# Gated-linear heads: the state update directly behind the scores, two stretches of projections per pair in place of three

## What is computed

```python
def gla_chunk(q, k, v, logf, s0):       # one chunk of L = 64 tokens
    b = jnp.cumsum(logf, axis=1)
    inter = jnp.einsum('blhk,bhkv->blhv', qf * jnp.exp(b), s0)
    decay = jnp.exp(jnp.where(causal, b[:, :, None] - b[:, None, :], -jnp.inf))
    attn = jnp.einsum('blhk,bmhk,blmhk->bhlm', qf, kf, decay)
    intra = jnp.einsum('bhlm,bmhv->blhv', attn, vf)
    k_dec = kf * jnp.exp(b_last[:, None] - b)
    s_new = jnp.exp(b_last)[..., None] * s0 + jnp.einsum('blhk,blhv->bhkv', k_dec, vf)
    return inter + intra, s_new
```

## Time and profile before

| | |
|---|---|
| median of three runs | 2609.63 us (2609.17 to 2614.47) |
| the profiled execution | 2610.18 us, of which its span is 2608.4 us |
| PE busy | 2502.8 us, 96% of the span |
| VectorE, ScalarE busy | 916.2 us (35%), 837.4 us (32%) |
| POOL busy | 552.7 us (21%) |
| granted TensorE clock | 0.986 of full speed on average |
| DMA | 53 GB/s over the span |

### The profile page before, as it was taken

How to read it: one execution, slowest core, us unless ns; L and a number is a source line. 1 busy time by engine, 2 the same in 40 slices (tenths; PEclk the granted TensorE clock), 3 DMA queues, 4 the chain that set the end, 5 groups by cost and what they waited for, 6 DMA issues and landing times.

```text
span 2608.4 us, 41617 instructions
## 1 busy us (share of the span) xinstructions
PE 2502.8 (96%) x17454; PEld 2363.0 (91%) x17454; DVE 916.2 (35%) x1793; ACT 837.4 (32%) x1658; POOL 552.7 (21%) x306
## 2 busy tenths in 40 slices
PE   6999999999999999999998999889999999999998
PEld 5888878798999999999997877688999999999997
DVE  6454454517322222222227344425422222222216
ACT  4445444536220221121125455536411211211212
POOL 1101110115221221211215210104312212211213
PEclk9999999999999999999999999899999999999999
DMA  3101010114111111111114100003211111111114
GB/s 108 41 10 48 22 44 17 44 45 150 61 45 41 48 40 48 40 48 40 53 40 141 62 26 26 30 27 121 84 41 49 40 48 40 48 40 41 47 53 134
DMA packets 63088, 139.05 MB, mean 53 GB/s; under 512 B 8688, under 2 KB 39920, under 8 KB 62960
## 3 DMA queue, kind: packets, MB, share of 16 engines
q1 hardware_dynamic: 33984, 103.60, 11.9%
q10 hardware_dynamic: 28976, 33.64, 4.2%
HBM read 117.81 MB, written 19.40 MB: 53 GB/s over the span
## 4 chain that ended last, share of the span: by engine, by line
PE 80%; DVE 3%; ACT 2%; issue 1%; ACTq 0%; DVEq 0%
PE banks L217 52%; PE banks L197 20%; PE banks L1903 1%; PE banks L1423 1%; PE banks L1404 1%; PE banks L1391 1%; PE banks L1431 1%; PE banks L2054 0%; PE banks L383 0%; PE banks L2057 0%; PE banks L2038 0%; ACT y L1557 0%; DVE y L614 0%; PE banks L1427 0%; PE banks L1385 0%
## 5 line engine op out<-in xcount | busy, mean ns | idle before, releaser
L160 POOL TENSOR_TENSOR w_lo<-w_raw,w_hi 128x1024 fp32r<-128x1024 f32 x168 | 414.9, 2473 | 1880.4 <-ACT w_hi L153 1880.4
L197 PE MATMUL banks<-h_hi,w_hi 128*128 128x384 f32 (+1 forms) x1224 | 430.0, 351 | 6.4 <-ACT gla_v_tok L2153 3.1
L197 PE MATMUL banks<-h_lo,w_hi 128*128 128x384 f32 (+1 forms) x1224 | 408.6, 334 | 0.0
L197 PE MATMUL banks<-h_hi,w_lo 128*128 128x384 f32 (+1 forms) x1224 | 408.2, 334 | 0.0
L153 ACT CAST w_hi<-w_raw 128x1024 fp32r<-128x1024 f32 x180 | 187.3, 1048 | 464.3 <-DMA w_raw<-in_units 464.0
L217 PE MATMUL banks<-h_hi,w_hi 128*128 128x384 f32 (+1 forms) x1368 | 301.7, 329 | 0.0
L217 PE MATMUL banks<-h_lo,w_hi 128*128 128x384 f32 (+1 forms) x1368 | 301.3, 328 | 0.0
L217 PE MATMUL banks<-h_hi,w_lo 128*128 128x384 f32 (+1 forms) x1368 | 301.3, 328 | 0.0
L217 PE MATMUL banks<-mlp_a_hi,w_hi 128*128 128x384 f32 (+1 forms) x1344 | 296.6, 329 | 1.5 <-issue 1.3
L217 PE MATMUL banks<-mlp_a_lo,w_hi 128*128 128x384 f32 (+1 forms) x1344 | 295.1, 327 | 0.0
L217 PE MATMUL banks<-mlp_a_hi,w_lo 128*128 128x384 f32 (+1 forms) x1344 | 295.0, 327 | 0.0
(11 more groups left out here) (201 smaller groups left out, 3175.9 us busy)
## 6 DMA issues: line engine op xcount, KB each, us to landing
w_raw<-in_units SPq DMA_DIRECT2D x180, 512.0 KB, 3.5
x_scratch<-y ACTq DMA_DIRECT2D x48, 192.0 KB, 2.0
norm_x<-x_scratch ACTq DMA_DIRECT2D x40, 192.0 KB, 2.6
x_scratch<-y ACTq DMA_DIRECT2D x24, 160.0 KB, 1.8
norm_x<-x_scratch ACTq DMA_DIRECT2D x20, 160.0 KB, 2.5
y<-in_x SPq DMA_DIRECT2D x16, 192.0 KB, 5.3
norm_x<-in_x ACTq DMA_DIRECT2D x16, 192.0 KB, 3.0
out_y<-y SPq DMA_DIRECT2D x16, 192.0 KB, 2.3
```

The source lines that it names most:

```text
L160: c.nc.gpsimd.tensor_tensor(c.w_lo[:, s], c.w_raw[:, s], c.w_hi[:, s].bitcast(F32), ALU.subtract).then_inc(self.ready, 1)
L197: mm = chip.nc.tensor.matmul(out, w, x, start=(first and n == 0), stop=(last and n == 2))
```

## The change

`update` moves directly behind `scores`; a pair has two stretches of projections, one between update and output and one behind the output. `STEPS`, `HIGHS` and ScalarE's places for `take_jobs` follow from that. On VectorE `states` moves from behind `differences(g + 2)` to directly behind `attention(g)`, and `output_variance` behind it.

```diff
-    PARTS = 3
+    PARTS = 2
-    STEPS = (PARTS * NPAIR, PARTS * NPAIR, PARTS * NPAIR, 21)
+    STEPS = (PARTS * NPAIR, PARTS * NPAIR, PARTS * NPAIR, 14)
-    HIGHS = ({2: 6, 4: 7, 10: 8, 15: 9}, {4: 4, 6: 5, 10: 6, 13: 7, 16: 8, 19: 9}, {4: 4, 6: 5, 10: 6, 13: 7, 16: 8, 19: 9},
-             {4: 4, 8: 5, 13: 6, 15: 7, 18: 8, 24: 9})
+    HIGHS = ({1: 6, 2: 7, 6: 8, 10: 9}, {2: 4, 4: 5, 6: 6, 8: 7, 10: 8, 12: 9}, {2: 4, 4: 5, 6: 6, 8: 7, 10: 8, 12: 9},
+             {2: 4, 5: 5, 8: 6, 10: 7, 12: 8, 16: 9})
...
                 scores(h, p)
+                update(h, p)
                 fill(h, self.PARTS * p)
-                update(h, p)
+                output(h, p)
                 fill(h, self.PARTS * p + 1)
-                output(h, p)
-                fill(h, self.PARTS * p + 2)
...
+                take_output(h, p)
+                if h and p == 0:
+                    scale_outputs(h, 2)
                 take_jobs(h, slot + 1)
                 if slot + 1 in self.HIGHS[h]:
                     ws.high(act, self.unit(h, self.HIGHS[h][slot + 1]))
-                take_output(h, p)
-                if h and p == 0:
-                    scale_outputs(h, 2)
-                take_jobs(h, slot + 2)
-                if slot + 2 in self.HIGHS[h]:
-                    ws.high(act, self.unit(h, self.HIGHS[h][slot + 2]))
...
                     nc.vector.memset(self.state[:, 0, 0], 0.0).then_inc(self.state_zero, 1)
-                    if h:
-                        output_variance(h)
+                states(h, p)
+                if h and p == 0:
+                    output_variance(h)
                 decayed(g + 1)
...
                 differences(g + 2)
-                states(h, p)
```

## The result

The changed kernel takes 2629.64 us (median of five runs, 2625.67 to 2634.69) against 2610.86 in the same comparison: 1.0071 times the kernel before, 95% interval 1.0059 to 1.0083. The direction was forecast, the size was not: +18.8 us where +6.6 was expected, outside the range of 2610.5 to 2622.

The account below looks back on a forecast made before the run. PE was taken as busy nearly throughout, waiting mainly at the scores (10.8 us) behind VectorE's and ScalarE's chain. Terms 3.6 + 1.6 + 1.6 - 0.55 + 1.7 - 1.4 = 6.55 gave 2616.2 us beside the median, range 2610.5 to 2622.

Parts of the forecast that it names:

- eight pairs ahead of a waiting scores group: Pairs 2, 3 (head 0), 4, 5 (heads 1, 2), 0, 1 (head 3): next scores 0.9 later, less savings, +3.6 us.
- three pairs with almost no slack: Pair 5 of head 0, pairs 4 and 5 of head 3: the later chain delays the next scores, +1.6 us.
- pair 0 of heads 1 and 2: Scores start with 0.1 us of slack after the output's reading; `states` and `output_variance` move ahead: 2 x 0.8 = 1.6 us.
- pair 1 of head 0, pair 2 of head 3: First: `states` runs during a VectorE stall, -0.7 us; second: output wait replaced by a wait through the exponentials, +0.15.
- pairs 1 and 2 of heads 1 and 2: Update waits for late key copy in pair 1, gate matmuls for `gated` in pair 2: 2 x 0.85 = 1.7 us.
- the pairs paced by PE: 17 pairs whose pace PE itself sets: each saves 0.08 us with update directly behind scores, -1.4 us in all.
- The saving of a joined group: On PE, update directly behind scores saves a group entry and exit: 0.08 us per pair, middle of 0 and 0.16.
- rival 3: PE's clock halves behind longer waits at two gate pairs and head 0's longest wait: up to +9.6 us, 2619.3; chance 0.15.
- Rivals 2 and 4: Update behind scores saves more: 2, 0.35 per pair, 2611.6 us, chance 0.24; 4, whole 0.82, 2603.7 us, chance 0.09.

Follow-up runs that it names:

- last experiment: Changed kernel with unneeded matmuls in PE's waits (3 at the gate) and `states` behind `gated` in pairs 1 and 2 of heads 1 and 2: 2615.44 us.
- fifth experiment: Changed kernel with unneeded 256-column matmuls where PE waits, ahead of thirteen pairs' scores and a gate matmul in heads 1 and 2: 2622.48 us, ratio 1.0051.
- sixth experiment: Changed kernel with `states` behind `gated`, still ahead of the differences, in pairs 1 and 2 of heads 1 and 2 alone: 2621.22 us, ratio 1.0049.

## Why the prediction was wrong

By its own terms, the profiled execution of the changed kernel against that of before, from head to head (sum 17.4):

| term | forecast | measured | in the last experiment |
|---|---|---|---|
| eight pairs ahead of a waiting scores group | 3.6 | 4.8 | 3.7 |
| three pairs with almost no slack | 1.6 | 1.7 | 1.7 |
| pair 0 of heads 1 and 2 | 1.6 | 2.1 | 2.1 |
| pair 1 of head 0, pair 2 of head 3 | -0.55 | -0.7 | -0.7 |
| pairs 1 and 2 of heads 1 and 2 | 1.7 | 5.4 | -2.4 |
| the pairs paced by PE | -1.4 | 4.1 | 0.9 |

**What was right.** The mechanism: `states` delays the differences, these the exponentials, and ScalarE's reading of the output bank behind them holds the next scores. The first four terms came out at 7.9, forecast 6.25; 1.1 of the difference is pair 1 of head 3, which ran at a mean clock of 0.79 and got 1.1 back with the added matmuls of the fifth experiment. The saving of a joined group was put at 0.08 and is 0.04 on average in the twelve undisturbed pairs, from 0.18 shorter to 0.11 longer. The gate matmul in pair 2 was freed 5.8 after the scores, 0.9 later than before, as said. The scan was freed of POOL's subtraction: pair 5 of heads 1 and 2 is 0.6 shorter.

**What failed: the last term.** "The 17 pairs that PE itself paces: -17 x 0.08". The step priced each wait at its own length and took these pairs to be untouched by waits ahead of them. Three of them ran at 1.2 GHz for a while behind a wait of 1.1 to 2.3 us: pair 4 of head 0 (+1.45), pair 6 of head 2 (+1.5), pair 3 of head 3 (+1.3). I had this as rival 3 with a chance of 0.15 and priced it at up to 3; the added matmuls of the fifth experiment give back 7.2 of the 18.8. The rest of the term's miss of 5.5 is pair 0 of head 0 (+0.4) and the saving, half of what I took. The clock should have stood in the sum: there are 28 us of waiting in sixteen places instead of 10.8 in nine, and the earlier trace rows had shown half clock behind an idle of 0.92. With the rule of the Trainium skill cited in the prediction (idle gaps drop the clock, the work behind pays) the runs agree in part: the clock fell behind eight of the changed kernel's waits and not behind others of the same length. That section of the Trainium skill does not say that gaps as short as these are enough. That it is the added waits which bring the clock down is inferred from the clocks of all executions: 0.977 to 0.981 in the changed kernel, 0.980 to 0.987 before.

**What failed: the fifth term.** In pairs 1 and 2 of heads 1 and 2 I priced the second gate matmul's wait and the late key copy, 1.7 for all four pairs; it was 5.4. The key copy was priced too high: the update waited 0.22 in pair 1 of each head, not 0.45 to 0.5. Missing were, first, the turned outputs of pair 1, which wait for a bank that `gated` frees. This is the wait in head 1, before and after:

```profile
216.28 0.55 PE L1946 MATMUL banks<-identity,gla_v_tok 128*128 128x128 f32 x3 [0.43 <-DVE y L2431]
```

```profile
223.57 0.55 PE L1946 MATMUL banks<-identity,gla_v_tok 128*128 128x128 f32 x3 [1.04 <-DVE y L2427]
```

The wait was there before, 1.4 in four places, though the earlier trace rows does not list it, and `gated` 0.9 later makes it longer; the sum has no term for it. Pair 1 of head 2 was as long (12.86) without this wait, at a mean clock of 0.87. Second, the lower clock behind the gate's wait, now in both heads:

```profile
236.23 1.45 PE L1922 MATMUL banks<-keep,gla_gate_w 32*128 32x384 f32 x4 [1.05 <-DVE y L2427]
...
238.06 0.52 PE L197 MATMUL banks<-h_lo,w_hi 128*128 128x384 f32 x1
238.38 0.52 PE L197 MATMUL banks<-h_hi,w_lo 128*128 128x384 f32 x1
```

The sixth experiment put `gated` ahead of the state and won 8.4, of which 3.0 in its profile is clock in pairs that it did not touch. It and the fifth overlap at the gate; together they win 14.2 (2629.6 to 2615.4; 15 by the ratios). What is left is 4.3 by the medians and 5.3 in the heads of the profile: 6.8 of the chain (the first four terms), -2.4 at the gate pairs, 2.0 of it because pair 2 of head 2 was slow in the profile of before, and 0.9 in the pairs paced by PE, where pair 4 of head 0 was still slow (+1.4).

**Also off:** pair 0 of head 0 was 0.4 longer, at the lower clock from before the heads; the idle time at L2000 was forecast to rise to some 20 us and rose to 28.0; and the wait at the output in pair 2 of head 3, which I read as 2.5, is an idle time of 1.87. Rivals 2 and 4 fell: they need 0.35 and 0.47 per joined group, and it saves 0.04. The forecast of 2616.2 is within 1 us of the last experiment, but that holds two errors of opposite sign (-2.4 where 1.7 stood, 0.9 where -1.4 stood): it is luck in part, and no proof of each term.

What stays open: why the median differs by 18.8 and this pair of profiles by 22.8 (the rest lies outside the heads), and what decides at which wait the clock falls.

## What to carry to other kernels

A wait that is removed at one group comes back at the next one if the instruction moved forward stands in a queue ahead of what the next group waits for; so list, for each instruction that is moved, all that it now stands ahead of, and follow the longest chain to the pacing engine. An instruction placed directly behind another gives up the time in which its own operands were prepared: the update was free there only as long as ScalarE happened to be idle. And price a wait of PE by more than its length where dense matmuls follow at PE's pace: here such a place cost some 1.5 us more when the clock fell behind it. When an order is written by hand for a loop whose passes differ, choose it pass by pass from the trace.

## What the runs showed of the hardware

The lower clock is worth several us here: the same changed kernel with 7 to 30 unneeded matmuls ahead of the scores of thirteen pairs, and 8 ahead of a gate matmul of two, runs 7.2 us faster, at a mean granted clock of 0.984 to 0.987 in place of 0.977 to 0.981. How long PE had idled does not tell whether the clock falls. In the profile of the changed kernel six pairs that opened behind an idle of 1.12 to 3.94 us ran at mean clocks of 0.79 to 0.88, and five that opened behind 1.10 to 2.19 us at 1.00. Pair 6 of heads 1 and 2 has the same instructions and the same idle before it (1.13 and 1.12), and took 12.29 and 13.80; pair 1 of these heads (2.12 and 2.13) ran at 1.00 and 0.87. Where the clock was low, dense matmuls of 384 columns started 0.32 us apart instead of 0.18. The added matmuls kept the clock full in four of five pairs of one kernel, and in two others slow stretches turned up behind them.
